# Two chained transformer blocks on one core: copying a bank half out early, moving modulation tiles, and reordering the begin of the wide feed forwards

## What is computed

```python
def swiglu(h, w_in, w_out):                      # layers 0 and 1
    gate, up = jnp.split(h @ w_in, 2, axis=-1)
    return (jax.nn.silu(gate) * up) @ w_out

def conv_ffn(h, w_up, conv_w, w_down):           # layers 2 and 3
    up = h @ w_up
    a, b = up[..., :D_FF_2], up[..., D_FF_2:]
    return (jax.nn.silu(dwconv3(a, conv_w)) * b) @ w_down

m = jax.nn.silu(cvec) @ w_ada + b_ada            # six modulation vectors for each layer
x = x + gt2 * conv_ffn(modulate_2(rmsnorm(x, g2), sh2, sc2), w_up, ffn_conv, w_down)
```

## Time and profile before

| | us |
|---|---|
| median of 3 runs | 3416.39 (3415.55 to 3424.51) |
| the profiled execution | 3418.2 |
| its span, first to last instruction | 3416.9 |
| PE busy | 3257.2 |
| DVE busy | 2137.8 |
| ACT busy | 1395.0 |
| POOL busy | 492.6 |

### The profile page before, as it was taken

How to read it: one execution, slowest core, us unless ns; L and a number is a source line. 1 busy time by engine, 2 the same in 40 slices (tenths; PEclk the granted TensorE clock), 3 DMA queues, 4 the chain that set the end, 5 groups by cost and what they waited for, 6 DMA issues and landing times.

```text
span 3416.9 us, 45016 instructions
## 1 busy us (share of the span) xinstructions
PE 3257.2 (95%) x17816; PEld 2775.8 (81%) x17816; DVE 2137.8 (63%) x3440; ACT 1395.0 (41%) x2241; POOL 492.6 (14%) x498
## 2 busy tenths in 40 slices
PE   6998989999999999999999999989999999999998
PEld 4787779999978888878888876878889887678887
DVE  3677477777765554558657466477777765654444
ACT  4567453333344334342223345353333353543323
POOL 0001132233310000003001000132223310010001
PEclk9999999999999999999999999999999999999999
DMA  5500114333421221226444211123333331122232
GB/s 208 220 22 2 38 68 130 122 110 131 129 92 49 96 75 52 89 70 202 166 147 150 88 38 50 50 76 124 116 99 124 127 98 62 44 80 97 92 101 81
DMA packets 98689, 334.39 MB, mean 98 GB/s; under 512 B 11872, under 2 KB 16768, under 8 KB 95024
## 3 DMA queue, kind: packets, MB, share of 16 engines
q1 hardware_dynamic: 77072, 252.63, 21.8%
q0 software_dynamic: 21408, 78.88, 7.2%
HBM read 329.37 MB, written 2.10 MB: 97 GB/s over the span
## 4 chain that ended last, share of the span: by engine, by line
PE 82%; DVE 11%; ACT 5%; issue 2%; DMA 0%; POOL 0%; DVEq 0%; ACTq 0%; POOLq 0%
PE PS L574 40%; PE PS L781 15%; PE PS L681 6%; PE PS L831 2%; PE PS L986 2%; PE PS L583 2%; PE PS L957 2%; DVE WL L1775 2%; PE PS L899 1%; PE PS L914 1%; PE PS L618 1%; DVE HL L1887 1%; PE PS L1101 1%; PE PS L887 1%; PE PS L1059 1%
## 5 line engine op out<-in xcount | busy, mean ns | idle before, releaser
L1172 ACT ACTIVATE WH<-WR 128x1024 fp32r<-128x1024 f32 (+3 forms) x520 | 445.6, 860 | 991.0 <-PE PS L574 754.3
L1775 DVE TENSOR_TENSOR WL<-WR,WH 128x1024 fp32r<-128x1024 f32 (+3 forms) x520 | 525.7, 1011 | 437.8 <-ACT WH L1172 437.3
L574 PE MATMUL PS<-HH,WH 128*128 128x512 f32 (+1 forms) x1544 | 527.2, 373 | 15.6 <-DVE WL L1775 13.4
L574 PE MATMUL PS<-HH,WL 128*128 128x512 f32 (+1 forms) x1544 | 523.3, 371 | 0.0
L574 PE MATMUL PS<-HL,WH 128*128 128x512 f32 (+1 forms) x1544 | 523.3, 371 | 0.0
L574 PE MATMUL PS<-D,WH 128*128 128x512 f32 (+1 forms) x1668 | 426.1, 361 | 0.1
L574 PEld LDWEIGHTS PS<-HH,WH 128*128 128x128 f32 x1544 | 270.1, 188 | 76.7 <-DVE WL L1775 17.5
L574 PEld LDWEIGHTS PS<-D,WH 128*128 128x128 f32 x1668 | 278.8, 188 | 52.6 <-DVE D L2175 1.8
L574 PEld LDWEIGHTS PS<-HH,WL 128*128 128x128 f32 x1544 | 270.4, 189 | 50.9
L574 PEld LDWEIGHTS PS<-HL,WH 128*128 128x128 f32 x1544 | 269.5, 189 | 51.0 <-issue 1.0
L574 PE MATMUL PS<-D,WL 128*128 128x512 f32 x834 | 260.1, 360 | 0.0
(11 more groups left out here) (369 smaller groups left out, 6455.9 us busy)
## 6 DMA issues: line engine op xcount, KB each, us to landing
WR<-in_win SPq DMA_DIRECT2D x176, 512.0 KB, 3.5
AT<-in_adat POOLq DMA_DIRECT2D x144, 512.0 KB, 3.9
WR<-in_wret SPq DMA_DIRECT2D x64, 512.0 KB, 3.7
WR<-in_zin SPq DMA_DIRECT2D x36, 512.0 KB, 3.5
WR<-in_wdn SPq DMA_DIRECT2D x32, 448.0 KB, 3.3
WR<-in_wdn SPq DMA_DIRECT2D x48, 256.0 KB, 2.6
WR<-in_wdn SPq DMA_DIRECT2D x32, 320.0 KB, 2.8
AR<-in_ada SPq DMA_DIRECT2D x8, 1024.0 KB, 9.7
```

The costliest lines, as they stand in the source:

```text
L574: mm = PE.matmul(dst[:, a:b], w(u)[:, k * P:(k + 1) * P], h[:, k, a:b], start=(k == 0 and i == 0), stop=(k == nk - 1 and i == 2))
L1172: AC.activation(M.hi(u), M.raw(u), COPY).then_inc(*on.up("w_hi", u))
L1775: VE.tensor_tensor(M.lo(u), M.raw(u), M.hi(u).bitcast(F32), ALU.subtract).then_inc(*on.up("w_lo", u))
```

## The change

1. `CHUNKS` is (5, 4, 4, 4, 5) in layers 0 and 2, and (7, 7, 8) in layers 1 and 3; `TAIL_AT` = 4 in all tails. Some SBUF tiles move.
2. `ada_slots`: in chunks 1 to 3 of the wide layers pairs j = 1 and 2 take two narrow tiles one behind the other, and down steps 6 and 7 take none.
3. Layer 2: product (j,3) is copied out of half A by ACT (`keep(j, 3)`), PE's (j+2,1) waits for that copy, and the two multiplies become one of 768 columns with all operands in SBUF (`conv_multiply`).
4. Begin of the wide feed forwards: the eight `whole` of the image come behind the first gate activation, `turned` 0 and 1 ahead of the multiply, the third `turned` moves from POOL to DVE, `turned_high` and `turned_low` in another order.
5. In the wide layers, but for the last chunk, the low part made behind down step 7 comes ahead of that step's addition to X.
6. POOL: the loop is written another way, with the same order of sums and issues; one more wait in `sums`.

```diff
-CHUNKS = ((5, 5, 4, 4, 4), (8, 7, 7), (5, 5, 4, 4, 4), (8, 7, 7))
+CHUNKS = ((5, 4, 4, 4, 5), (7, 7, 8), (5, 4, 4, 4, 5), (7, 7, 8))
+TAIL_AT = 4
+WIDE_DOWN = (0, 4, 4, 3)
...
         for j in range(3 if ch == 0 else 0, nj):
-            at["up", ch, j] = (next(narrow),)
-        for m in range(1 if ch < 3 else 0, KT if ch < 4 else 0):
-            at["down", ch, m] = (next(wide if ch < 2 or (ch == 2 and m in (2, 4)) else narrow),)
+            at["up", ch, j] = tuple(next(narrow) for _ in range(1 + (0 < ch < 4 and j in (1, 2))))
+        for m in range(0 if ch else 1, KT - 2 if ch < 4 else 0):
+            at["down", ch, m] = (next(wide if ch == 0 or m in (1, 3, 4, 5)[4 - WIDE_DOWN[ch]:] else narrow),)
...
-        if g == 1 and v == 0 and k == (3 if tag == "3a" else 4) and not context_first(tag):
+        if g == 1 and v == 0 and k == TAIL_AT and not context_first(tag):
...
-                    PE.wait_ge(*on("up_half", (l, jj - 2, 1)))
+                    PE.wait_ge(*(on("up_half", (l, jj - 2, 1)) if l == 0 else on("kept", (l, jj - 2, 3))))
...
-            dst = {1: HF[:, 0:Q], 6: SG[:, 0:Q], 5: SG[:, Q:T]}[i]
+            dst = {1: HF[:, 0:Q], 6: SG[:, 0:Q], 5: SG[:, Q:T], 3: HF[:, Q:T]}[i]
...
-            if i in (1, 5, 6):
+            if i in (1, 5, 6) or i == 3 and l > 0:
                 keep(j, i)
...
         else:
+            keep(j, 3)
             refill(FIRST["down", l, ch] + 1)
             conv_silu(j)
...
-            whole(f"{l}b", l, [(0, k) for k in range(KT)] + [(1, k) for k in range(4)])
+            whole(f"{l}b", l, [(0, k) for k in range(KT)])
...
-                if l in HALVED and jj:
-                    turned_high(l, 1)
-                    turned_high(l, 2)
...
+                if l in HALVED and jj == 0:
+                    whole(f"{l}b", l, [(1, k) for k in range(KT)])
                 refill(W.after(u, 3))
-                if l in HALVED and jj == 0:
-                    whole(f"{l}b", l, [(1, k) for k in range(4, KT)])
...
                 if l in HALVED and jj == 0:
+                    turned_high(l, 1)
+                    turned_high(l, 2)
                     turned_high(l, 0)
...
+        def conv_multiply(j):
+
+            SG, HF, _ = place(j)
+            VE.wait_ge(*on("gate_silu", (l, c0 + j)))
+            VE.wait_ge(*on("kept", (l, c0 + j, 3)))
+            VE.wait_ge(*on("joined", (l, c0 + j, 2)))
+            VE.tensor_tensor(HF[:, :], SG[:, :], HF[:, :], ALU.mult).then_inc(*on.up("up_half", (l, c0 + j, 1)))
...
                 if i == 2 and j > js[0]:
-                    multiply(j - 1, 0)
-                    multiply(j - 1, 1)
+                    conv_multiply(j - 1)
...
+                if l in HALVED and jj == 1:
+                    turned_low(l, 2)
+                    turned_low(l, 0)
...
-                refill(W.after(u, 3))
+                if l in HALVED and jj == 0:
+                    turned(l, 0)
+                    turned(l, 1)
+                else:
+                    refill(W.after(u, 3))
...
                 if l in HALVED and jj == 0:
-                    turned(l, 0)
-                    turned(l, 1)
+                    refill(W.after(u, 3))
+                    turned(l, 2)
                     turned(l, 3)
...
                 if l in HALVED and jj == 0:
-                    for t in range(3):
-                        turned_low(l, t)
+                    turned_low(l, 1)
...
+                turn = l in HALVED and ch < LAST[l] and m == KT - 1
+                if turn:
+                    refill(W.after(first + m, 2))
                 down(l, ch, m, segs, PS[m % 2 if m else 2])
-                refill(W.after(first + m, 2))
+                if not turn:
+                    refill(W.after(first + m, 2))
...
         PO.wait_ge(*on("w_sum", (u, 5)))
+        if before is not None:
+            PO.wait_ge(*on("w_lo", (before, 6)))
...
-                PO.wait_ge(*on("h_whole", (f"{l}b", 1, KT - 1)))
-                PO.tensor_tensor(M.XF[:, 2], M.TF[:, 4:8, Q:T], M.TF[:, 0:4, Q:T], ALU.subtract).then_inc(*on.up("t_sum", l))
+                PO.wait_ge(*on("t_raw", (l, 3)))
                 sums(up + 2 * js[0])
```

More of the change, by code:

```diff
@@ L267, in feed_forward @@
         self.D1 = t("D1", [P, 2, 8, S], F32R)
-        self.DH = [self.D2[:, :, 0, :] if segments(l) == ALL else self.D1[:, 0, :, :] for l in range(4)]
-        self.DL = [self.D2[:, :, 1, :] if segments(l) == ALL else self.D1[:, 1, :, :] for l in range(4)]
+        self.top = stage + 12 * 1024
+        self.D3 = t("D3", [P, 8, 2, T], F32R)
+        tiles = [self.D2 if l in HALVED else self.D3 if segments(l) == ALL else self.D1 for l in range(4)]
+        self.DH = [d[:, 0, :, :] if d is self.D1 else d[:, :, 0, :] for d in tiles]
+        self.DL = [d[:, 1, :, :] if d is self.D1 else d[:, :, 1, :] for d in tiles]
         self.top = stage + 60 * 1024
@@ L442, in piece, with kept @@
     return (tag, k, g) if k in sum(tail_tiles(tag), ()) else (tag, k)
+def kept(tag):
+    return tag in [f"{l}b" for l in HALVED]
 def norm_tiles(M, tag):
-    if tag in ("0b", "2b"):
+    if kept(tag):
         return M.FRI, M.FRS
@@ L1877, in scaled @@
         at = KT * g + k
-        if at > 4 and tag not in ("0b", "2b"):
+        if at > 4 and not kept(tag):
             VE.wait_ge(*on("h_lo", (tag, (at - 5) // KT, (at - 5) % KT)))
@@ L2136, in halves @@
             refill(FIRST["down", l, ch] + 1)
-            multiply(j, 0)
-            multiply(j, 1)
+            conv_multiply(j)
             conv_low(j)
@@ L2651, in sums, with feed_forward @@
         PO.tensor_tensor(M.SF[2][:, :], up[:, H:2 * H], M.SF[1][:, :], ALU.subtract).then_inc(*on.up("w_sum", (u, 3)))
-    def feed_forward(l, ada):
+    def feed_forward(l):
+        ada = l + 1
         slots, n = ada_slots(ada), 2
+        if l not in HALVED:
+            PO.wait_ge(*on("h_lo", (f"{l}b", 1, KT - 1)))
+            for v in range(NV):
+                modulation(ada, v)
+            return
         for ch, nj in enumerate(CHUNKS[l]):
@@ L2664, in feed_forward @@
                 modulation(ada, 1)
-            for j in js:
-                if j > js[0]:
-                    sums(up + 2 * j)
-                if ("up", ch, j - 1) in slots:
+            for j in range(js[0], nj):
+                if j < nj - 1:
+                    sums(up + 2 * (j + 1))
+                for v in slots.get(("up", ch, j), ()):
                     modulation(ada, n)
                     n += 1
-            if ("up", ch, nj - 1) in slots:
-                modulation(ada, n)
-                n += 1
             for m in range(KT):
@@ L2676, in feed_forward @@
                     sums(FIRST["up", l, ch + 1])
-                if ("down", ch, m) in slots:
+                for v in slots.get(("down", ch, m), ()):
                     modulation(ada, n)
@@ L2711, in pool_program @@
     squares("0b", T)
-    feed_forward(0, 1)
+    feed_forward(0)
     PO.wait_ge(*on("d_lo", (0, LAST[0], CHUNKS[0][-1] - 1)))
@@ L2727, in pool_program @@
         if l == 2:
-            feed_forward(2, 3)
+            feed_forward(2)
         PO.wait_ge(*on("d_lo", (l, LAST[l], CHUNKS[l][-1] - 1)))
```

17 lines of the change are left out of this document (10 added, 7 removed).

## The result

The changed kernel takes 3425.13 us (median of 8 runs, 3421.97 to 3426.76), the kernel before 3415.97 on the same chip: ratio 1.0025, interval 1.0014 to 1.0036. By the ratio it is some 8.5 us slower (9.2 by the two medians), where 2.1 faster was forecast. The profiled execution has a span of 3424.1, 7.2 above that of before.

What follows compares the result with a forecast made beforehand. PE, busy for 95% of the span, was taken as the bound, so only its idle time could be won. From 3418.2, -7.3 + 20 - 9.2 - 2.5 - 2.9 - 0.2 = -2.1, less 1.8 for the median: 3414.3 us, range 3391 to 3431.

Steps and rivals of the forecast that it cites:

- The direction: Whole kernel: 2.1 us faster than before, at a chance of 0.50 for the forecast.
- Part 2, the doubled tiles, first layer: First layer, chunks 1 to 3: two tiles in a section land late and PE waits, 6.65 a chunk, +20 us.
- the forecast's loop: First layer's sections with two tiles: issue, landing and DVE's work close a loop of 18.5 us against PE's 14.75.
- Part 2, third layer: Third layer, chunks 1 to 3: doubled tiles lose 3.1 us for j=2 and 0.35 for j=1, 5.05 a chunk in all.
- Part 1, the copy: Third layer's loop: PE's wait for the multiply goes (28.6 us), a loop of 16.2 keeps 21.3, net -7.3.
- rival C: Third layer: the loop through D low and ACT's copy is as long as before, copy gives 0; 3421.6 us, chance 0.08.
- The lock: Third layer: joint multiply contends with POOL for shared ports, holding POOL 0.4 longer in 10 sections, 4 us; not in the sum.
- Part 3, chunk ends: Wide layers' chunk ends: earlier low part and no tile there close six PE gaps a layer, 4.6 each layer, -9.2 us.
- Part 4, begins: Begins of the wide feed forwards: new order of ACT and DVE work gives -2.5 us in the first layer, 0 in the third.
- Part 5, ends: Layer ends: larger last chunks cover more of the last square sum's wait, first layer 1.3, -2.9 us in all.
- Rival B: Both wide layers: late tiles plus POOL's sums stretched, each late tile 1.2 later; +16.0, 3432.4 us, chance 0.18.
- Rival A: Late tiles cost only 9 us and the third layer's loop gives 18; -23.8, 3392.6 us, chance 0.24.

Runs made afterwards that it cites:

- e2_early: The changed kernel with POOL issuing the modulation tiles of a pair ahead of the sums for the next pair; 3396.70 us, ratio 0.9938 to the kernel before.
- e3_double: The kernel before with only the changed kernel's places of the tiles (doubled tiles, none behind down steps 6 and 7), POOL's order kept; 3443.75 us, ratio 1.0080.
- e4_copy: The kernel before with only the third layer's part: ACT's copy of (j,3), PE's wait for it, joint multiply; 3400.85 us, ratio 0.9950.
- e12_down: e2_early with the six extra tiles of chunks 1 to 3 behind down steps 0 and 2 instead of in pairs 1 and 2; 3402.69 us.
- e9_nocopy: The changed kernel without the third layer's part (ACT's copy, joint multiply); 3437.81 us, ratio 1.0071 to the kernel before.
- e11_split: e2_early with the third layer's joint multiply as two of 384 columns, both from SBUF; 3398.54 us, ratio 0.9958 to the kernel before.
- e6_lowfirst: The kernel before with only the low part behind down step 7 moved ahead of that step's addition; 3424.23 us, ratio 1.0019.
- e5_begin: The kernel before with only the new order at the begin of the wide feed forwards; 3412.05 us, ratio 0.9986.

## Why the prediction went wrong, point by point

**The direction.** Forecast -2.1, measured +8.5. The time lies in the range, within 0.3% of before, but it moved the other way. The sum was made of a loss of 20 and gains of 22, so a few us decide the sign. In the profiled executions 9.3 are missing (+7.2 for -2.1), and 7.6 of them lie in the third layer's feed forward.

**Part 2, the doubled tiles, first layer: right, +20 forecast, 21.0 measured** (e2_early against the changed kernel), 19.2 in e3_double. The mechanism is shown: one exchange of two steps on POOL takes it away. Its inside was not as told. There are four gaps of PE, not nine (4.57, 2.52 and 2.57, 4.47; 14 us). Around them the granted clock is 0.50, and the four sections, 20.8, 18.9, 19.0 and 21.6 long, are 1.6, 1.8, 1.9 and 2.6 longer than the gap and the 14.57 of a section without one: some 8 us of clock, which the forecast did not count here. That the sum came out at 20 is in part luck: fewer gaps than forecast, and clock in their place. (The terms of the forecast's loop, as written, sum to 18.8, not 18.5.) Landing was taken at 3.9. Two tiles asked for together can be later: the first issue of the pair in chunk 1 is at 595.94 and DVE has it at 601.22, 5.3 later. In chunk 3 it was 4.05, so this is not the reason for every gap.

**Part 2, third layer: the failed step.** The forecast put the doubled tiles there into part 1: 5.05 a chunk (0.35, 3.1 and 1.6) where two sections with one tile lose some 3, so about 2 a chunk over the plain loop. Measured, a chunk of e4_copy less its own gap at the begin is 95.6 (96.32 - 0.74), and the changed kernel's is 101.4 in the mean. So the doubled tiles cost 5.8 a chunk there instead of 2, 11 us more in three chunks. That is near what they cost in the first layer (7.0 a chunk): the forecast let the price of the tiles take the place of what the loop loses anyway, 3.1 instead of 1.45 to 1.6, where the runs show it added nearly in full. DVE's timeline in the changed kernel shows two waits for AT with a tile's 1.2 behind each, all ahead of the low part, and then PE's gap behind that:

```profile
2497.16 1.23 DVE L1820 SCALAR_TENSOR_TENSOR AT<-AT,CB 128x1024 f32<-128x1024 f32 x1 [0.57 <-DMA AT<-in_adat]
...
2499.71 1.23 DVE L1820 SCALAR_TENSOR_TENSOR AT<-AT,CB 128x1024 f32<-128x1024 f32 x1 [1.31 <-DMA AT<-in_adat]
...
2500.86 0.69 DVE L1787 TENSOR_TENSOR WL<-WR,WH 128x512 fp32r<-128x512 f32 x1
```

```profile
2501.60 0.44 PE L793 MATMUL PS<-XH,WH 128*128 128x384 f32 x1 [2.60 <-DVE WL L1787]
```

The section from (2,1) to (3,1) takes 18.9, 20.9 and 21.8 in the changed kernel, 17.2 in e2_early and 15.0 to 15.1 in e4_copy. Taking the lateness away gives back 3.0 of the 5.8 a chunk. The other 2.8 (98.4 in e2_early) are not the second tile's own time alone: e12_down gives 0.7 to 1.7 for that. A likely part of the rest, which no run isolates, is D's low part: in e2_early POOL's sums stand beside it and stretch it for two of the four pairs of a chunk:

```profile
2389.83 2.03 DVE L2112 TENSOR_TENSOR D<-WK,D 128x768 fp32r<-128x768 f32 x1
```

In e4_copy it is short for every pair of chunks 1 to 3:

```profile
2395.62 0.95 DVE L2100 TENSOR_TENSOR D<-WK,D 128x768 fp32r<-128x768 f32 x1
```

In the changed kernel it is stretched once only, so its 5.8 may be made up in another way than 2.8 and 3.0. How they divide there stays open.

**Part 1, the copy: mechanism right, gain too small.** The section of 16.2 came at 16.18 and 16.22, the wait for the multiply is gone, and the part is worth 17 alone and 16 in the changed kernel. The forecast's -7.3 holds 6 for the tiles; without them it is some -13.5, and the rest is clock that isn't lost. That it should fail (rival C) is refuted by e4_copy and e9_nocopy.

**The lock.** The joint multiply takes 0.95 alone and 2.05 beside POOL's sums, a modulation tile 1.22 and 2.33. These traces agree with what the Trainium skill says on the page "SBUF — State Buffer", section "Who interferes with whom": a DVE instruction with two SBUF inputs contends with a GpSimd instruction that reads SBUF. The +4 that the prediction derived from it did not turn the part into a loss: it is worth 16 to 17 with the multiply held in ten places. The joint form is also better in the traces than two short multiplies from SBUF (e11_split), since each of those waits for itself.

**Part 3, chunk ends: -9.2 forecast for two edits, and the work is mostly that of the free steps.** The low part's new place alone is +6.5 (e6_lowfirst). With both, the gaps are closed in both layers: from a chunk's first matmul to (1,1) PE takes 10.4 instead of 12.2 (chunks 1 and 2) and 11.3 (chunks 3 and 4), 5.4 a layer, where 4.6 was forecast. How much of it the third layer keeps behind that, where its loop over DVE sets the pace, no run separates.

**Part 4, begins: -2.5 forecast, -4.8 measured** (e5_begin): within its bounds.

**Part 5, ends: the first layer's -1.3 is there** (4.21 to 2.83). The chunk sizes alone cost 6, mostly by a gap that the prediction hadn't looked for and that the changed kernel's places of the tiles avoid, and by two falls of the clock that come with the sizes.

**Rival B** named what happened in sign, slower by the tiles, with the wrong price: it had sums of POOL stretched in both layers. **Rival A**'s 3392.6 is near what e2_early gives, 3396.7, but that comes by taking the lateness away rather than by slack.

**What stays open.** +4.5 between the two wide feed forwards and -1.8 and -2.1 outside them are mostly stretches at half clock at places whose instructions did not change (next section). Of the +4.5, 3.4 are the two falls that come with the new chunk sizes; why the sizes of chunks in a feed forward change the clock in a mixer was not settled.

## What to carry to other kernels

When a consumer takes two items in one slot, both loads have to be asked for a whole slot earlier. So when tiles are moved on the consumer's side, look at what stands ahead of the issue on the issuing engine: exchanging that order cost nothing here and was worth 28 us. Where the delayed engine is already in the loop that sets the pace, add the delay to what the loop loses; don't let one take the place of the other. A slow instruction costs only when there is no slack ahead of it: the same tile of 2.33 stood in two kernels, once with a gap of 0.72 behind it and once with 2.59. And a small edit may be worth something only beside another one; run alone, two parts of this change were losses, by gaps that the whole does not have.

## What the runs showed of the hardware

The granted clock need not answer alike to the same wait. In the mixer of the third layer PE is busy without a break for more than 16 us at granted clock 1.00 in both kernels, and then waits 1.27 us for the same instruction, at 1997.73 before and at 2010.12 after:

```profile
2010.12 0.47 PE L595 MATMUL PS<-HH,WH 128*128 128x512 f32 x1 [1.27 <-ACT DV L1663]
```

The stretches behind it, the kernel before and then the changed one:

```profile
1997.73:2001.00 3.27, 3.27 (x17) 2.52 (x19) 2.31 (x5) 1.77 (x4) 0.00 (x0) 1.00 0.48 160
```

```profile
2010.12:2013.50 3.38, 3.38 (x12) 2.74 (x12) 2.30 (x5) 1.89 (x4) 0.00 (x0) 0.59 0.49 155
```

At full speed 17 matmuls in 3.3 us, and 12 at a mean of 0.59. A fall lasts some 3.4 us in most places and 6.8 or more in others, and costs half of that where PE is busy all through it. Over the whole span (stretches of 1 us, each by the part of the clock that was not granted) it is 39 us in the profiled execution before, 39 in the changed one and 29 in e2_early; some of it falls on time in which PE was idle anyway. A count of gaps therefore gives the time of a kernel like this one no closer than by a few us.

Modulation DMAs of 512 KB take 3.9 us to land in the median. Of two issued one behind the other in the changed kernel, DVE, where it waited, had the first 3.7 to 4.1 us after its issue, and 5.3 in one case (601.22). Where it waited for the second, it had that 6.4 to 7.3 us after the first issue (703.04, 2399.00, 2499.71, 2602.69).

DVE instructions of 1024 columns with two SBUF inputs take 1.22 us alone and up to 2.33 beside POOL's sums, those of 768 columns 0.95 and 2.05. POOL's sums take 1.3 alone and up to 2.3 beside them.
